# Attention by query tile between the value-projection matmuls, the HGRN output inside the attention, and the first sums of the output projection ahead of the HGRN norm (1 core)

## The reference, cut to what matters

```python
proj = jnp.einsum('bsd,de->bse', rmsnorm(h, norm1_w), w_in)
qa, ka, va = ...            # attention: 8 heads of 64
qb, fb, ib, gb = ...        # HGRN: 4 heads of 128
# attention: three dilated windows (128,1), (512,4), (2048,16), their softmaxes joined by their lse weights
y = sum(weights * outs)
# HGRN2: o = intra-chunk + inter-chunk part, then
o = o * lax.rsqrt(jnp.mean(o * o, axis=-1, keepdims=True) + NORM_EPS)
yb = o * norm_w * jax.nn.silu(g)
h = h + jnp.einsum('bse,ed->bsd', concat([ya, yb]), w_out)
```

## Time and profile before

| | us |
|---|---|
| median of 3 runs (lowest, highest) | 2258.04 (2256.44, 2258.2) |
| the profiled execution's own time | 2256.9 |
| its span | 2255.1 |
| PE busy in the span | 2164.3 |
| DVE busy | 1521.4 |
| ACT busy | 1073.4 |
| POOL busy | 234.9 |

### The profile page before, as it was taken

How to read it: one execution, slowest core, us unless ns; L and a number is a source line. 1 busy time by engine, 2 the same in 40 slices (tenths; PEclk the granted TensorE clock), 3 DMA queues, 4 the chain that set the end, 5 groups by cost and what they waited for, 6 DMA issues and landing times.

```text
span 2255.1 us, 25922 instructions
## 1 busy us (share of the span) xinstructions
PE 2164.3 (96%) x8736; PEld 1432.9 (64%) x8736; DVE 1521.4 (67%) x1575; ACT 1073.4 (48%) x950; POOL 234.9 (10%) x239
## 2 busy tenths in 40 slices
PE   8999999999999999999999999689997899999998
PEld 3445457777777777777777777445643346888886
DVE  3953369999999999999999999544614633333333
ACT  1010147777777777777777777420002423222222
POOL 0003311112111111121211211100000000000000
PEclk9998989999999999999999999889998899999999
DMA  6123379999999999999999999611221011222220
GB/s 255 56 84 114 121 317 340 377 376 382 376 374 381 373 384 373 382 379 373 384 372 381 382 370 380 254 38 38 94 93 47 1 38 56 94 94 98 108 94 37
DMA packets 77756, 522.63 MB, mean 232 GB/s; under 512 B 10208, under 2 KB 10736, under 8 KB 21264
## 3 DMA queue, kind: packets, MB, share of 16 engines
q1 hardware_dynamic: 65088, 483.95, 55.4%
q0 software_dynamic: 9168, 31.01, 5.4%
q10 hardware_dynamic: 3456, 7.06, 1.0%
HBM read 500.98 MB, written 18.99 MB: 231 GB/s over the span
## 4 chain that ended last, share of the span: by engine, by line
PE 90%; DVE 7%; ACT 1%; DMA 1%; issue 1%; SPq 0%; DVEq 0%; ACTq 0%; POOLq 0%
PE bank L1006 21%; PE bank L1008 21%; PE bank L1007 21%; PE bank L872 13%; PE bank L1118 6%; DVE room L1301 3%; PE bank L1022 1%; PE bank L1133 1%; PE bank L1216 1%; PE bank L978 1%; PE bank L1014 1%; PE bank L881 1%; PE bank L1198 1%; DVE room L1640 1%; DVE room L1662 0%
## 5 line engine op out<-in xcount | busy, mean ns | idle before, releaser
L1448 DVE TENSOR_TENSOR ring_r<-ring,room_r 128x2048 fp32r<-128x2048 f32 x384 | 873.3, 2288 | 90.1 <-ACT room_r L626 87.3
L626 ACT ACTIVATE room_r<-ring 128x2048 fp32r<-128x2048 f32 x384 | 735.7, 1917 | 189.0 <-PE bank L1008 183.3
L1006 PE MATMUL bank<-room_r 128*96 128x512 f32 x1536 | 607.1, 395 | 3.5 <-DVE room_r L1480 1.9
L1008 PE MATMUL bank<-room_r 128*96 128x512 f32 x1536 | 603.1, 393 | 0.0
L1007 PE MATMUL bank<-ring_r,room_r 128*96 128x512 f32 x1536 | 603.0, 393 | 0.0
L1008 PEld LDWEIGHTS bank<-room_r 128*96 128x96 f32 x1536 | 248.8, 162 | 105.7
L1006 PEld LDWEIGHTS bank<-room_r 128*96 128x96 f32 x1536 | 248.9, 162 | 105.4 <-DVE ring_r L1448 4.4
L1007 PEld LDWEIGHTS bank<-ring_r,room_r 128*96 128x96 f32 x1536 | 249.0, 162 | 101.0 <-issue 0.2
L872 PE MATMUL bank<-ring,room 128*128 128x512 f32 x544 | 238.9, 601 | 4.0 <-ACT room L587 3.3
L872 PEld LDWEIGHTS bank<-ring,room 128*128 128x128 f32 x544 | 104.7, 194 | 134.5 <-issue 133.5
L1118 PE MATMUL bank<-room,ring 128*128 128x512 f32 x320 | 140.4, 597 | 0.0
(11 more groups left out here) (243 smaller groups left out, 2053.8 us busy)
## 6 DMA issues: line engine op xcount, KB each, us to landing
ring<-in_wmoe SPq DMA_DIRECT2D x384, 1024.0 KB, 11.6
ring<-in_wf SPq DMA_DIRECT2D x33, 1024.0 KB, 4.8
ring<-in_wp SPq DMA_DIRECT2D x9, 2048.0 KB, 7.8
ring<-in_wd SPq DMA_DIRECT2D x7, 2048.0 KB, 8.9
ring<-in_wd SPq DMA_DIRECT2D x3, 1024.0 KB, 8.1
room<-in_xT SPq DMA_DIRECT2D x2, 1024.0 KB, 8.4
room<-in_xtok ACTq DMA_DIRECT2D x1, 2048.0 KB, 7.7
h_rows<-room POOLq DMA_DIRECT2D x4, 512.0 KB, 3.1
```

The source lines that it names most:

```text
L626: act.activation(w_hi[s_ % PAIRS], raw_w[ORDER[s_]], ACT.Copy)\
L1006: pe.matmul(out, x_hi, w_hi, start=start, stop=False, skip_group_check=True)
L1008: return pe.matmul(out, x_lo, w_hi, start=False, stop=stop, skip_group_check=True)
L1448: dve.tensor_tensor(w_lo[i], raw_w[i], w_hi[s_ % PAIRS].bitcast(F32), ALU.subtract)\
```

## The change

- **Value tiles.** The 64 matmuls are issued one at a time (`vt_step`, into banks 6 and 7): 16 ahead of the attention, 8 after the first four `scores`, and 40 in units 0 to 22, four in each of units 0 and 1 and then two and one in turn (`VT_STEPS`). ACT copies a tile out in the unit in which it ends (`VT_DONE`).
- **Attention by query tile.** A unit's transposes go side by side into one bank (2 or 3 in turn), ACT copies them in one instruction, and `values(u)` multiplies unit by unit, two units after `probs_T(u)`. `masked` and the exponential now run four units ahead.
- **Counts in the mask.** The table added by `masked` holds log(count)/scale; the sum of the exponentials comes from the exponential's own accumulator on ACT. Lines 1654 and 1662 go. The reduction takes the minimum of the negated, scaled scores.
- **HGRN output.** `hgrn_out(j)` computes one token tile, tokens on partitions (4(j+1) matmuls 128x128, bank 6), at the start of units 24, 26, 28 and 30. ACT copies it and squares each head's 128 columns with a sum (`hgrn_evac`, 5 instructions). After the attention ACT takes one root of 128x16, DVE one reciprocal of 128x16 and two products of 128x1024; PE transposes (`hgrn_turn`, 16 blocks), DVE multiplies by the gate (4 products of 128x512). The norm's weight is multiplied into the gate already at the input projection, at the same place as before (one op instead of another).
- **Output projection.** 8 banks. Tiles 0 to 4 sum the first three of eight steps (attention, heads 0 to 5) before the transposes of the HGRN output, then the fourth, then the HGRN half; tiles 5 to 7 follow whole.
- **DMA.** The table of constants is a quarter smaller. The third piece of feed-forward weights waits for the last `hgrn_turn`; the row of the final norm is loaded after the seventh piece. Two semaphores are merged into another.

```diff
+VT_STEPS = [3 * KT, 3 * KT + 4, 4 * KT] + [4 * KT + (3 * n + 1) // 2 for n in range(1, 22)] + [8 * KT] * 9
+VT_DONE = [next(u for u in range(HEADS * TT) if VT_STEPS[u + 1] >= KT * (g + 1)) for g in range(3, 8)]
+O_AT = [24, 26, 28, 30]
...
+            def probs_out(u):
+                i = u % TT
+                act.wait_ge(s["pt_ready"], u + 1)
+                if u >= TT:
+                    act.wait_ge(s["pv_ready"], u - TT + 1)
+                act.activation(pTa[i], bank[2 + u % 2][:, 0:(i + 1) * P], ACT.Copy).then_inc(s["pt_evac"], 1)
...
+            def hgrn_evac(j):
+                act.wait_ge(s["o_ready"], j + 1)
+                act.activation(on[:, j, :], bank[6][:, :], ACT.Copy)
+                for h in range(HG_HEADS):
+                    n = j * HG_HEADS + h
+                    ins = act.activation(junk[:, h * P:(h + 1) * P], bank[6][:, h * P:(h + 1) * P], ACT.Square, accum_out=hms[:, n:n + 1])
+                ins.then_inc(s["o_evac"], 1)
...
+            vt_out(0)
+            vt_out(1)
+            for u in range(AHEAD):
+                exps(u)
+            vt_out(2)
             for u in range(HEADS * TT):
                 h, i = divmod(u, TT)
-                act.wait_ge(s["sc_done"], u + 1)
...
+                probs_out(u)
+                if u + AHEAD < HEADS * TT:
+                    exps(u + AHEAD)
                 if i == 2 and h >= 1:
-                    probs_out(h - 1)
-                if i == TT - 1 and h >= 1:
                     head_out(h - 1)
-            probs_out(HEADS - 1)
+                if u in VT_DONE:
+                    vt_out(3 + VT_DONE.index(u))
+                if u in O_AT:
+                    hgrn_evac(O_AT.index(u))
+            act.wait_ge(s["o_evac"], TT)
+            act.activation(hms, hms, ACT.Sqrt, bias=eps_rms, scale=1.0 / P).then_inc(s["ostd_ready"], 1)
             head_out(HEADS - 1)
...
+            def hgrn_out(j):
+                pe.wait_ge(s["vt_evac"], 8)
+                pe.wait_ge(s["lv_copied"], LEVELS + 1)
+                if j >= 1:
+                    pe.wait_ge(s["o_evac"], j)
...
+            for n in range(2 * KT):
+                vt_step(n)
+            pe.wait_ge(s["rot_done"], 8)
+            pe.wait_ge(s["p_evac"], 8)
             for u in range(AHEAD):
                 scores(u)
+            for n in range(2 * KT, 3 * KT):
+                vt_step(n)
             for u in range(HEADS * TT):
+                for n in range(VT_STEPS[u], VT_STEPS[u + 1]):
+                    vt_step(n)
+                if u in O_AT:
+                    hgrn_out(O_AT.index(u))
+                if u >= 2:
+                    values(u - 2)
                 probs_T(u)
                 if u + AHEAD < HEADS * TT:
                     scores(u + AHEAD)
-                if u % TT == TT - 1:
-                    head_values(u // TT)
...
+            for g in range(5):
+                w_out(g, 3, 4)
+            pe.wait_ge(s["hmix_ready"], TT)
+            for g in range(5):
+                w_out(g, 4, KT)
+            for g in range(5, 2 * TT):
+                w_out(g, 0, KT)
...
+            for u in range(AHEAD):
                 masked(u)
+            weighted(0)
+            weighted(1)
             for u in range(HEADS * TT):
-                if u + AHEAD - 2 < HEADS * TT:
-                    masked(u + AHEAD - 2)
-                weighted(u)
+                if u + 2 < HEADS * TT:
+                    weighted(u + 2)
+                if u + AHEAD < HEADS * TT:
+                    masked(u + AHEAD)
```

More of the change, by code:

```diff
@@ L262, in build @@
         c2 = slot(3)
[L263 removed]
+        madd, cosT, sinT = (c2[:, n * S:(n + 1) * S] for n in range(1, 4))
         lmask = c2[:, 4 * S:4 * S + 8 * P].bitcast(I32).rearrange("p (l s) -> p l s", l=8)
@@ L754, in _, with vt_out @@
                            .then_inc(swap_in[m % 2], 16)
-            for g in range(8):
+            def vt_out(g):
                 act.wait_ge(s["vt_ready"], g + 1)
[L758 to L761, removed]
                 if g == 0:
                     act.wait_ge(s["lv_ready"], LEVELS + 1)
[L765 to L776, removed]
@@ L779, in probs_out @@
[L779 to L786, removed]
+                act.activation(v_tok[:, g, :] if g < 4 else i_tok[:, g - 4, :], bank[6 + g % 2][:, :], ACT.Copy)\
+                   .then_inc(s["vt_evac"], 1)
@@ L1165, in _ @@
-            pe.wait_ge(s["lv_copied"], LEVELS + 1)
-            pe.wait_ge(s["vt_evac"], 8)
-            def hgrn_out(h):
-                if h >= 2:
-                    pe.wait_ge(s["osq_ready"], h - 1)
-                for j in range(TT):
-                    ins = pe.matmul(bank[2 + h % 2][:, j * P:S], i_tok[:, j, h * P:(h + 1) * P], AT[:, h, j, j * P:S],
-                                    start=(j == 0), stop=(j == TT - 1), skip_group_check=True)
-                ins.then_inc(s["o_ready"], 1)
@@ L1176, in hgrn_ms @@
[L1176 to L1190 removed]
+                ins = pe.matmul(bank[6 + g % 2][:, :], uT[:, k, i * P:(i + 1) * P], w[:, k, :], start=(k == 0), stop=(k == KT - 1))
@@ new lines, in vt_step @@
+                if k == KT - 1:
+                    ins.then_inc(s["vt_ready"], 1)
+            def hgrn_out(j):
[3 more added lines that the diff above has]
+                    pe.wait_ge(s["o_evac"], j)
+                for h in range(HG_HEADS):
+                    for q in range(j + 1):
+                        ins = pe.matmul(bank[6][:, h * P:(h + 1) * P], AT[:, h, q, j * P:(j + 1) * P],
+                                        i_tok[:, q, h * P:(h + 1) * P], start=(q == 0), stop=(q == j), skip_group_check=True)
+                ins.then_inc(s["o_ready"], 1)
@@ L1192, in scores, with hgrn_turn @@
+            def hgrn_turn(j):
+                pe.wait_ge(s["on_ready"], j // 2 + 1)
+                if j >= 2:
+                    pe.wait_ge(s["hmix_ready"], j - 1)
+                for h in range(HG_HEADS):
+                    ins = pe.transpose(bank[6 + j % 2][:, h * P:(h + 1) * P], on[:, j, h * P:(h + 1) * P], ident)
+                ins.then_inc(s["oT_ready"], 1)
             def scores(u):
@@ L1218, in head_values, with w_out @@
                 ins.then_inc(s["pv_ready"], 1)
+            def w_out(g, first, last):
+                i, n = divmod(g, 2)
+                w = chunk2(pe, 7 + n).rearrange("p (k c) -> p k c", k=KT)
+                for k in range(first, last):
+                    ins = pe.matmul(bank[g][:, :], mixed[k][:, i * P:(i + 1) * P], w[:, k, :], start=(k == 0), stop=(k == KT - 1),
+                                    skip_group_check=True)
+                if last == KT:
+                    ins.then_inc(s["o2_ready"], 1)
@@ new lines, in _ @@
+            dve.wait_ge(s["ostd_ready"], 1)
+            step(dve.reciprocal(hms, hms))
+            for q in range(2):
+                part = on[:, 2 * q:2 * q + 2, :].rearrange("p j (h c) -> p (j h) c", h=HG_HEADS)
+                dve.tensor_tensor(part, part, hms[:, 8 * q:8 * q + 8].unsqueeze(2).broadcast_to([P, 8, P]), ALU.mult)\
+                   .then_inc(s["on_ready"], 1)
+            for j in range(TT):
+                dve.wait_ge(s["oT_ready"], j + 1)
+                dve.tensor_tensor(mix_hg[:, :, j * P:(j + 1) * P], bank[6 + j % 2][:, :].rearrange("p (h t) -> p h t", h=HG_HEADS),
+                                  hG[:, :, j * P:(j + 1) * P], ALU.mult).then_inc(s["hmix_ready"], 1)
```

153 lines of the change are left out of this document (67 added, 86 removed).

## The result

The changed kernel takes 2224.39 us (median of 4 runs, 2223.7 to 2224.99), the kernel before 2258.12 beside it: a ratio of 0.9855, with a 95% interval of 0.9844 to 0.9867, or 33.7 us less. 2222.8 was forecast, with a range of 2211 to 2236.

The account below looks back on a forecast made before the run. PE bounds the kernel, losing time where it idles or its clock drops. Its work, starts and waits in the changed stages sum to 186.9 against 222.1 us: gain 35.2 from 2256.9, 2221.7, plus 1.1 for the median, 2222.8; range 2211 to 2236.

Parts of the forecast that it names:

- 889998899: Clock digits per slice of the old profile, read as the only long weak part, near the end, where the changed stages are.
- the value tiles: Value-tile stage on PE: the same 64 matmuls, 55.1 us, only in other places.
- waits in `hgrn_out`: HGRN output's single bank: PE waits for ACT's copy and squares, 1.2, about 1.5 and 1.3, 4.0 us; bounds 0 and 6.
- rival B: Attention units 23 to 31, without value tiles: PE pauses, the clock falls; time 2231 to 2238; chance 0.20.
- the turns: PE's transposes of the HGRN output: 16 blocks and four starts 2.3, about 0.5 of waits, 2.8 us.
- At no price: Gate's product, third weight piece's later load and final norm's row, claimed to cost nothing.
- rotation: First scores wait on the last rotation, hidden by 16 value matmuls (13.7 us); without them it would cost 10.8 us.
- the norm: HGRN norm on DVE and ACT after the attention, about 5 us, hidden beside 14.4 us on PE; uncovered it costs 5.
- The chain of a unit: Attention unit's scores, mask, exponential, scaling: 3.5 us within three whole units of at least 1.5 us; nothing waits.
- A: Group starts on PE hidden behind long matmuls: half to all of 16 us gone, time 2207 to 2217; chance 0.16.
- D: Interleaving does nothing as ACT's copies hold PE back; only the HGRN output gains, 10 us, time 2248; chance 0.05.
- C: Clock stays at 1.2 GHz through the interleaved stretch, PE pausing at every group: time 2321; chance 0.04 with other upsets.

Follow-up runs that it names:

- experiment 1: Changed kernel with all value tiles ahead of the attention (last 8 matmuls right after the first scores), none in the units: 2219.2 us, ratio 0.9833.
- 3: Changed kernel with the table of counts back on DVE (two more DVE ops a unit) and no sum on ACT: 2226.12 us.
- 6: Changed kernel with both all value tiles ahead of the attention and the table of counts back on DVE: 2219.68 us.
- 5: Changed kernel with the wait on the last rotation and the first four scores ahead of all value tiles: 2240.7 us.
- 4: Changed kernel without output-projection sums ahead of the HGRN norm: last values, then turns, then all eight projection tiles whole: 2232.14 us.
- 7: Kernel of 6 with DVE's old order and lookahead too: masked(u+2) ahead of weighted(u): 2221.54 us.
- 12: Changed kernel with value tiles ahead, two HGRN output banks, that output in units 6, 12, 18, 24, and PE, ACT, DVE steps paired by two units: 2211.06 us.
- 9: Kernel of experiment 1 with the HGRN output in a stage of its own between value tiles and first scores: 2266.01 us, ratio 1.0042 to the kernel before.
- 10: Kernel of 9 with eight 128x512 matmuls, result unused, added right behind the first four scores: 2229.15 us.

## Why the prediction was right

*The bound.* PE's own work at the full clock, with its waits, was the right account: 186.9 us forecast for the stages up to the last output-projection matmul, 190.1 measured (1656.74 to 1846.83, the last instruction group's start at 1843.40 and eight times 0.43). The value of the sum rests on distances between starts of one head, and each held to 0.02 us. Against 222.1 before, that is 32.0 us gained of the 35.2 forecast. The medians say 33.7, nearer to the forecast than the traces have it: luck of about 2 us, no more than the spread. One reading was wrong and harmless: of the digits 889998899 the first two stand for the pause between the blocks (1409 to 1522 us), not for the changed stages, which begin at 1657.

*Mis-sized: the value tiles.* "The same 64 matmuls, 55.1 us, only in other places" left out that each group now pays a start: by distances between starts 59.4 against 55.1 us in experiment 1, with 24 groups against 2, so 22 more at 0.19, or 4.3. I had counted the starts of all other groups and not of these; experiment 1 measured 5.2 for the whole, a fall of the clock included that it did not have.

*Mis-sized: waits in `hgrn_out`.* 4.0 forecast, 0.52 + 1.54 + 0.60 = 2.7 found. ACT took 1.5 us for the copy and four squares, not 2.0: the read of a sum starts 0.16 behind its square and the next square 0.09 behind that. On the other side the clock fell once in the profiled execution (rival B in small), for 3.4 us, which cost 1.6. The first scores took 2.6 where 3.4 had been counted, the turns 2.5 in place of 2.8. The errors partly cancel, which is luck too: 4.3 + 1.6 - 1.3 - 0.8 - 0.3 leaves 3.5, against the 3.2 of the sum.

*At no price.* Counts (3, 6), rotation (5) and the norm (4) were indeed hidden, and so were the moved loads, as far as the equal length of the feed-forward part (375.1) shows it; no run moved them back. What the rotation costs uncovered I had put too low, since idle time also costs clock: 14.4 in the stretch and 16.3 by the medians, not 10.8. For the norm it is 5.3 in the stretch and 7.7 by the medians, where I had 5.

*The chain of a unit* fits into the lookahead, as the prediction had it ("nothing waits"), and with more room than it gave: with DVE's two ops and the old lookahead back, 7 lost only 2 us against 6, and most of that to the clock.

*The rivals.* A fell: starts do not vanish behind wide matmuls, and the value tiles paid them as well. What the Trainium skill says of weight loads pulled ahead (TensorE: Matmul & The Clock Gate, Part 2) holds within a group here and not at a change of kind: in a group the second load starts 0.42 us ahead of its matmul (1722.27 and 1722.69), but the first load of the next group starts with its matmul, at 1724.07. 12 measured 0.16 for each change. D fell with experiment 1. C did not come in the changed kernel, but its mechanism is real: 9 shows it, 92 us at 1.2 GHz. It was named, at 0.04, for the wrong reason: not small pauses between groups, since in 9 there are none while the clock is low, but larger pauses just ahead of the stream (1.8, 1.8, 1.8 and 1.5 us), after which a stream of short matmuls did not bring the clock back.

*Where the gain came from.* First, on PE. Before, it waits 24.8 us in the HGRN output and the attention, mostly here:

```profile
PE bank L1207 <- DVE room L1665: 7.3, 13, 0.8
PE bank L1216 <- ACT room L785: 5.6, 5, 1.5
PE bank L872 <- ACT room L773: 5.3, 2, 3.6
PE bank L1198 <- DVE att_s L1654: 4.2, 1, 4.2
```

In the changed kernel 3.1 of such waits are left. PE's own instructions, by distances between starts, went from 197.3 to 187.2, although they pay some 8 us of new starts (3.7 for the values, 4.3 for the value tiles): before, those of the attention took 73.2 us, where eight heads at the rate of the earlier trace rows are 55.4. So about 18 us of the gain is an attention that no longer runs at 1.2 GHz, and 22 are waits. The 18 is an estimate.

Second, by the parts of the change. With the interleaving, the counts and the new lookahead undone (7), the whole gain is still there, so it lies in the form by query tile, the HGRN output and the order of the output projection; no run has the form by query tile alone. The counts in the mask would have given 13 us alone and give under 2 beside it; the interleaving costs 5. How the 33.7 us divide between the form and the HGRN output's new place was not measured apart: 9 lost its comparison to the clock. Rid of that spell, as in 10, and of the 6.9 us added there, a serial HGRN stage would stand at about 2222 to 2224, 3 to 5 above 1; so its reciprocals of 3.36 us and matmuls with ones would be what cost time before, and its place only as far as its pauses pull the clock down. This is an estimate.

## What to carry to other kernels

Add up the in-order engine's work with a start for every group, also for the groups that are only moved: a filler interleaved one or two instructions at a time pays its own start, and if the ring does not wait it is a loss. An edit's worth depends on what bounds the loop at that time: price it on the new loop, not on the chain of the old one. Where a stage consists of short matmuls, look at the pauses just ahead of it and at the clock in its first units, and move or fill the pauses, or put wide work behind them.

## What the runs showed of the hardware

- The same stream of 128- to 512-column float32 matmuls, without a pause, ran at 2.4 GHz up to the HGRN output and past it (experiment 1) and for 92 us at 1.2 GHz (experiment 9). What differs is the place of the HGRN output: with pauses of 1.8 us and just ahead of the stream in 9, with pauses of at most 1.5 us and within it in 1; and 1 has a value tile behind the first scores. The low clock cost 41 us.
- The start of a group of another kind of matmul costs PE 0.15 to 0.2 us at the full clock, and about 0.18 at 1.2 GHz too (experiment 9); a semaphore wait that is already met inside a run of one kind costs nothing that shows (value tiles in a row in experiment 1, with a wait at each tile from the third on: 0.43 us an instruction).
- After one pause of 1.5 us in the HGRN output the clock fell in some executions of the same instructions and not in others: it fell for 3.4 us in the changed kernel and experiment 5, and not in 4, whose PE instructions are the same in these units.
- A square of 128 columns with its sum costs ACT 0.25 us from start to start.
